# The tail of an attention block: VectorE's and ScalarE's pieces moved two to four heads behind TensorE's, and the squares in a buffer of their own

## The reference, cut to what matters

```
for l in range(2):
    proj = x @ w_in                                  # q, k, v of both head groups
    o_diff = 8 heads: (softmax(q0 k0 + t5) - lam * softmax(q1 k1 + t5)) @ v
    o_diff = o_diff * rsqrt(mean(o_diff^2 over 64) + eps) * g * (1 - lam_init)
    o_na   = 8 heads: softmax(q k + window bias) @ v       # 2-D window, 256 keys here
    h = concat(o_diff, o_na) @ w_out                       # 1024 x 1024
    x = layer_norm(alpha * x + h)       # (x - mean) * rsqrt(var + eps) * g + b
    f = peer(x)                         # top-16 x top-16 key retrieval, expert sums
    x = layer_norm(alpha * x + f)
```

## Time and profile before

| what | us |
|---|---|
| median of 3 runs | 3393.82 (3392.39 to 3395.72) |
| the profiled execution, its own time | 3396.41 |
| its span in the trace | 3394.6 |
| PE busy over the span | 3167.8 (93%) |
| DVE busy | 2480.7 (73%) |
| ACT busy | 1233.7 (36%) |
| POOL busy | 1090.5 (32%) |
| mean granted TensorE clock | 0.969 |
| heads and tails of layer 1's attention | 175.3 to 382.6 in the trace |

### The profile page before, as it was taken

How to read it: one execution, slowest core, us unless ns; L and a number is a source line. 1 busy time by engine, 2 the same in 40 slices (tenths; PEclk the granted TensorE clock), 3 DMA queues, 4 the chain that set the end, 5 groups by cost and what they waited for, 6 DMA issues and landing times. The chain is left out here.

```text
span 3394.6 us, 48838 instructions
## 1 busy us (share of the span) xinstructions
PE 3167.8 (93%) x16726; PEld 2800.1 (82%) x16726; DVE 2480.7 (73%) x5112; ACT 1233.7 (36%) x1756; POOL 1090.5 (32%) x684
## 2 busy tenths in 40 slices
PE   7988799899899999999889888998999999999996
PEld 6866589898899999988677665898998999998885
DVE  3166389898688878778732654898978888787886
ACT  2365233344333333333223652333433333333332
POOL 0030056400355545433200301572004555454331
PEclk9989899999999999999999998999999999999998
DMA  7651225354999989889675422254569999898995
GB/s 260 139 131 60 89 83 175 134 235 187 364 347 349 347 319 340 308 316 352 218 268 126 113 81 76 97 174 166 193 235 365 360 340 336 317 343 287 338 353 180
DMA packets 334924, 806.17 MB, mean 237 GB/s; under 512 B 39312, under 2 KB 195472, under 8 KB 300208
## 3 DMA queue, kind: packets, MB, share of 16 engines
q1 hardware_dynamic: 258384, 525.31, 45.4%
q0 software_dynamic: 73728, 268.47, 21.2%
q10 hardware_dynamic: 2656, 10.49, 0.8%
HBM read 711.38 MB, written 99.09 MB: 239 GB/s over the span
## 5 line engine op out<-in xcount | busy, mean ns | idle before, releaser
L183 POOL DMA_INDIRECT g_ring<-in_peer_u,g_idx x256 | 365.4, 1427 | 793.8 <-DVE g_ring L193 744.4
L246 PE MATMUL o_bank<-v_hi,w_hi 128*128 128x512 f32 x1536 | 599.4, 390 | 16.5 <-DVE w_lo L1644 16.5
L247 PE MATMUL o_bank<-v_lo,w_hi 128*128 128x512 f32 x1536 | 600.4, 391 | 0.0
L248 PE MATMUL o_bank<-v_hi,w_lo 128*128 128x512 f32 x1536 | 600.2, 391 | 0.0
L183 POOL DMA_INDIRECT g_ring<-in_peer_v,g_idx x256 | 374.7, 1464 | 503.5 <-DVE x_sb L201 448.4
L1629 DVE TENSOR_TENSOR v_lo<-v_raw,v_hi 128x2048 fp32r<-128x2048 f32 x128 | 293.0, 2289 | 137.8 <-ACT v_hi L1564 137.4
L1564 ACT CAST v_hi<-v_raw 128x2048 fp32r<-128x2048 f32 x128 | 244.9, 1913 | 405.7 <-PE o_bank L248 386.4
L246 PE MATMUL h_bank<-x_hi,ws_hi 128*128 128x384 f32 x1152 | 385.7, 335 | 4.5 <-PEq L1312 4.5
L248 PE MATMUL h_bank<-x_hi,ws_lo 128*128 128x384 f32 x1152 | 385.7, 335 | 0.0
L247 PE MATMUL h_bank<-x_lo,ws_hi 128*128 128x384 f32 x1152 | 385.3, 334 | 0.0
L201 DVE SCALAR_TENSOR_TENSOR x_sb<-g_ring,g_h,x_sb 128x1024 f32<-128x1024 f32 x256 | 328.3, 1282 | 53.5 <-DMA g_ring<-in_peer_v,g_idx 36.3
(11 more groups left out here) (197 smaller groups left out, 6055.6 us busy)
## 6 DMA issues: line engine op xcount, KB each, us to landing
ws_raw<-in_uT SPq DMA_DIRECT2D x128, 1024.0 KB, 5.2
v_raw<-in_peer_v SPq DMA_DIRECT2D x128, 1024.0 KB, 6.9
gates_T<-gate_stage SPq DMA_DIRECT2D x12, 4096.0 KB, 12.6
g_raw<-gates_T SPq DMA_DIRECT2D x128, 384.0 KB, 8.9
w_raw<-in_w_in SPq DMA_DIRECT2D x24, 1024.0 KB, 9.2
ws_raw<-hidden_T SPq DMA_DIRECT2D x56, 384.0 KB, 4.7
w_out_half<-in_w_out SPq DMA_DIRECT2D x32, 512.0 KB, 3.5
ws_raw<-in_peer_wq SPq DMA_DIRECT2D x16, 1024.0 KB, 5.6
```

Source lines behind the costliest of these rows:

```text
L183: nc.gpsimd.indirect_dma_start(out=tail.ring[n % RING][:, :], out_offset=None, in_=table.rearrange("l e d -> (l e) d"), in_offset=bass.Ind ...
L246: nc.tensor.matmul(out, lh, rh, start=start, stop=False)
L247: nc.tensor.matmul(out, lh, rl, start=False, stop=False)
L248: return nc.tensor.matmul(out, ll, rh, start=False, stop=stop)
```

## The change

It changes the slots of all the pieces, gives the squares a place of their own at the end of the tile `t5_tables` (before, they were written into `heads_outT`, which the transposed heads also use), takes the squares for the LayerNorm in two instructions of 512 elements with a semaphore wait between them, adds one small VectorE instruction that adds their two sums, and changes the waits that go with the buffers. Pieces of TensorE move by 1 or 2 steps, those of VectorE and ScalarE by 1 to 6.

```
-        sq = catT[:, 0:DC // 2, :].rearrange("p c (h d) -> p (c h) d", d=HD)
+        squares = tb[:, NDH * T5_W:NDH * T5_W + NDH * HD]
+        sq = squares.rearrange("p (h d) -> p h d", d=HD)
-        mv = m.sb("ln_mv", [P, 2])
+        mv = m.sb("ln_mv", [P, 3])
...
-        MULS = {f"mul_{n}": u for n, u in enumerate((24, 25, 26, 27, 29, 30, 31, 32))}
-        PE_SLOTS = {"turn_na": 20, "turn_diff": 23, **MULS}
-        ACT_SLOTS = {"square": 18, "turn_na": 21, "turn_diff": 24, "spread": 33}
-        DVE_SLOTS = {"read_diff": 18, "read_na": 19, "sums": 20, "gain": 22, "add_0": 28, "add_1": 33, "spread": 35,
-                     "norm": 37}
-        POOL_SLOTS = {"sums": 20, "spread": 35}
+        MULS = {f"mul_{n}": u for n, u in enumerate((26, 27, 28, 29, 31, 32, 33, 34))}
+        PE_SLOTS = {"turn_na": 21, "turn_diff": 24, **MULS}
+        ACT_SLOTS = {"square": 20, "turn_na": 23, "turn_diff": 26, "spread": 39}
+        DVE_SLOTS = {"read_diff": 19, "read_na": 20, "sums": 22, "gain": 24, "add_0": 32, "add_1": 37, "spread": 40,
+                     "norm": 42}
+        POOL_SLOTS = {"sums": 22, "spread": 40}
...
                 if piece == "square":
                     act.wait_ge(o_read[0], qt + 1)
                     if qt >= 1:
-                        act.wait_ge(spread, qt)
+                        act.wait_ge(rms_asked, qt)
+                    if qt >= 2:
+                        act.wait_ge(spread, 2 * (qt - 1))
...
                     if i == 0:
-                        act.wait_ge(rms_asked, qt + 1)
+                        if qt >= 1:
+                            act.wait_ge(hid, 2 * PIECES * qt)
...
                     else:
                         if qt >= 1:
-                            act.wait_ge(spread, qt)
+                            act.wait_ge(hid, 2 * PIECES * qt)
...
                 if piece == "spread":
                     act.wait_ge(centred, qt + 1)
-                    nc.scalar.activation(catT[:, :, :].rearrange("p a b -> p (a b)"), x[:, qt, :], ACT.Square,
-                                         bias=mv[:, 0:1], accum_out=mv[:, 1:2]).then_inc(spread, 1)
+                    act.wait_ge(rms_asked, min(qt + 2, TT))
+                    for i in range(2):
+                        if i == 1:
+                            act.wait_ge(spread, 2 * qt + 1)
+                        nc.scalar.activation(squares, x[:, qt, i * 512:(i + 1) * 512], ACT.Square, bias=mv[:, 0:1],
+                                             accum_out=mv[:, 1 + i:2 + i]).then_inc(spread, 1)
...
                 if piece == "spread":
-                    dve.wait_ge(spread, qt + 1)
+                    dve.wait_ge(spread, 2 * (qt + 1))
+                    chain.done(nc.vector.tensor_scalar(mv[:, 1:2], mv[:, 1:2], mv[:, 2:3], None, ALU.add))
+                    chain.wait()
```

## The result

The changed kernel takes 3370.2 us (median of 6 runs, 3363.1 to 3375.56), the kernel before 3393.4 beside it (6 runs): a ratio of 0.993 with a 95% interval of 0.9917 to 0.9943, 23.2 us less. The forecast was 3369.5 within 3361 to 3386. The profiled execution took 3368.03 (span 3366.3), 28.4 less than the profiled one of before.

A forecast was written before the change was run, and what follows sets the result against it. TensorE paces where muls stand, VectorE elsewhere. Per layer 10.1 up to add_1 of block 2 + 3.0 after the last head - 0.6 last LayerNorm = 12.5, 25.0 for both; this gave 3368.8, stated as 3369.5, range 3361 to 3386.

The forecast's parts named there:

- The block: One block of 16 heads, transpose 13 to the same point a block later: 42.4 us instead of 46.8, 4.4 less.
- Behind the gain: At position 8, TensorE waits for VectorE's gain and maxima 9': a new wait of 1.9 us per block.
- Behind the norm: At position 10, TensorE waits for VectorE's norm and maxima 11': a wait of 2.3 us per block.
- The end: After the last head: gain 3.8 behind add_1 instead of 6.8, norm hidden behind the 16 muls; gains 3.0 per layer.
- last LayerNorm: On the path at each layer's end: two halves 1.66 instead of 1.28, small addition 0.2; costs 0.6 (bounds 0.2 and 1.5).
- add_1 of block 2: After the blocks of a layer: 10.1 us earlier, at 340.5 instead of 350.66.
- the 1.6 at the start of block 1: No earlier LayerNorm there; moving reads and sums one or two steps spares 1.6 us net of the later mul.
- Rival 1: The clock falls in the new gaps, slowing muls: 7 to 14 us over four transitions, 3376 to 3383; chance 0.2.
- the forecast's own signs of being wrong: Gain and norm waits together over 6 us, granted clock 0.50 while muls 0 to 3 run, or a mul awaiting a transfer.
- Rival 2: VectorE's chain takes it all back: block stays near 46.8, only the end gains, 3.0 - 0.6 per layer: 3389; chance 0.11.
- Rival 3: Slower: TensorE waits out every insertion up to the norm, 7.7 us a transition instead of 6.5: 3403; chance 0.06.
- The edits priced at nothing: The buffer for squares and its waits cost nothing: they wait on muls that ended three or more steps earlier.

The follow-up runs named there:

- the repeat: The changed kernel run once more, unchanged, as the measure for the others of its set: 3369.88 us, ratio 0.9931.
- halves only: The kernel before with its old slots, plus the squares' new buffer, the halves, the small addition and their waits: 3396.86 us, ratio 1.0017.
- norm first: The changed kernel with block 2's norm put directly behind its spread, ahead of block 3's gain: 3375.77 us, ratio 0.9946.

## Why the prediction was right

**The block.** 42.8 us instead of the forecast 42.4, from 46.8. The waits behind the adds are gone, as the forecast's bookkeeping had them, and its reason, the adds' place, is what the experiments bear out: add_0 alone in the old layout -14.9, the adds back near their muls +11.4, +8.6 and together +23.9. That it is the distance alone is shown for add_0 only.

**The new waits.** Behind the gain 1.75 for 1.9. Behind the norm 0.63 for 2.3: the place was right, the size was not, because the clock was low just ahead. The times of resuming agree, 6.06 us from one wait's end to the next (269.00 to 275.06) for a forecast 5.92, and the repeat, with full clock there, shows 2.48.

**The end.** Gain to add_1 3.84 for 3.8, first mul 2.72 behind the gain for 2.73, last LayerNorm +0.7 for +0.6. POOL's power took 1.64 us where nothing of the norm lay beside it, 1.66 in the earlier trace rows, where the norm began 0.56 us before its end, and 2.63 beside the norm in the old layout, in the run with the halves only too. This is the rule of the Trainium skill's GPSIMD Engine Reference (Specifications) on SBUF interfaces shared with VectorE, and the trace agrees in sign.

**Sizes that were off.** Over the stretch the forecast's 12.5 a layer became 13.2 in layer 1 and 12.5 in layer 2, 25.7 for 25.0. In layer 1 add_1 of block 2 came 9.4 earlier for 10.1 (10.9 less the 1.5 that lie ahead of transpose 13), since each block is 0.4 longer than forecast. The last 16 muls gave 1.5 that the forecast had left as it was: first mul to second add 15.5 instead of 17.0, since less of them ran at 1.2 GHz (mean granted clock 0.90 instead of 0.82). Two small waits that it had not named stand in the traces: 0.43 at 217.78, where the values wait for the first read, and 0.88 at 340.62 (turn_na behind add_1). The other 2.7 of the 28.4 in the profiled pair lie in parts that the change does not touch. The medians show 23.2, 1.8 less than the sum; the low clock on the muls, 2.4 us in the repeat, is part of such a difference. That the median was hit within 1 us is in part luck: the parts that nobody changed move by several us from one execution to the next. One term of the forecast, the 1.6 at the start of block 1, comes without its working, and the traces can't be read for it alone, since the adds stand at other heads now.

**The rivals.** Rival 1 is partly true: low clock at 271 and 312 in the first trace, at 274 on the muls in the second (2.4 us). That is one of the forecast's own signs of being wrong, a granted clock of 0.50 while muls 0 to 3 run; it cost 2.4 us in one transition where the rival had up to four such, and did not decide. With both adds near it came in three of four. Rival 2, only the end gains, falls with the block period. Rival 3 falls: it had 7.7 us of waits a transition, and the block shows 2.4. The edits priced at nothing, the buffer and its waits, were not measured alone in the changed kernel; in the old layout they cost 5.2 together with the halves, for which the forecast had 0.6 a layer.

**What is not settled.** One instruction of 1024 elements with a buffer of its own would tell the halves' price in the changed kernel; it wasn't tried. Nor is it settled why the low clock falls behind the gain in one execution and on the muls in the next. The parts don't add up exactly, as each was measured in another layout: 20 to 24 for the adds, 5.9 for the order at the end, -5.2 for the halves, 21 to 25 against 23.2.

## What to carry to other kernels

Where one in-order engine feeds another in short rounds, put the instruction that waits on a long producer behind enough of the work that the producer itself needs next; one or two steps were worth 20 us here, at no change in work. Mind what else stands behind the waiting instruction: the read of the next heads was held up along with the maxima. Price a stall by the difference of start times across it with and without, not by the idle time in brackets: 1.65 shown were 2.2 lost, and 2.1 were 2.6. Compare a change over the stretch that it touches, from a point ahead of it, when the rest of the kernel scatters by more than the parts you want to tell apart. When steps move, look at the transfers too, since a long load ahead of a short one on the same queue is a wait that appears only once the engine is fast enough.

## What was new about the hardware

- GpSimd's power of 128x8 took 1.64 us here and 2.63 beside the norm's two-input VectorE instructions; the small one of 128x1 took 0.54, 0.93 or 1.55. Three of them, each from another kernel (halves only, changed, norm first):

```profile
354.66 0.54 POOL L741 TENSOR_TENSOR ln_rs<-ln_rs,minus_half 128x1 f32<-128x1 f32 x1 [38.43 <-DVE ln_rs L903]
```
```profile
343.79 0.93 POOL L741 TENSOR_TENSOR ln_rs<-ln_rs,minus_half 128x1 f32<-128x1 f32 x1 [0.55 <-DVE ln_rs L905]
```
```profile
343.93 1.55 POOL L743 TENSOR_TENSOR ln_rs<-ln_rs,minus_half 128x1 f32<-128x1 f32 x1 [0.55 <-DVE ln_rs L907]
```

  The longest lies beside the norm from its start on, the middle one beside the gain's end and the norm's start, the shortest beside a small reciprocal and a read. It goes the other way too: in the repeat of the changed kernel the norm's first instruction, 1.28 us in the first trace, took 1.72 with a GpSimd instruction of two inputs starting beside it at 271.16:

```profile
271.14 1.72 DVE L910 SCALAR_TENSOR_TENSOR x_sb<-x_sb,ln_mv,ln_params 128x1024 f32<-128x1024 f32 x1
```
- A wait of 1.75 us was followed within 2 us by a stretch at 1.2 GHz in one execution and not in the next, at the same place of the same kernel (269.00 and 268.57). What the low clock cost depended on the pacer: nothing visible where VectorE was, 2.4 us where the muls were. "TensorE: Matmul & The Clock Gate" in the Trainium skill (What's actually happening) has activity release the half-rate state; that fits both, and by itself doesn't say which of the two a gap brings.
- A part of 512 KB landed in 3.6 us (median), but in 7.4 to 9.3 issued behind the load of 2048 KB, which itself took 8.3 to 10.5.
